# Experts gathered in pairs by 256-column products, and a down projection whose first unit waits for fewer hidden pairs

## What is computed

```python
def swiglu(h, w_in, w_out):
    g, u = jnp.split(jnp.einsum('bld,df->blf', h, w_in), 2, axis=-1)
    return jnp.einsum('blf,fd->bld', jax.nn.silu(g) * u, w_out)

def moe_swiglu(h, w_router, w_exp_in, w_exp_out):
    logits = jnp.einsum('bld,de->ble', h, w_router).astype(jnp.float32)
    top_v, top_i = lax.top_k(logits, TOP_K)
    gates = jax.nn.softmax(top_v, axis=-1)
    ...
    for e in range(N_EXPERTS):
        y = y + dense_gate[..., e:e + 1] * swiglu(h, w_exp_in[e], w_exp_out[e])
```

## Time and profile before

| What | us |
|---|---|
| median of 3 runs | 1950.88 (1950.7 to 1952.35) |
| the profiled execution: its own time | 1948.23 |
| its span, first to last instruction | 1946.5 |
| PE busy in the span | 1838.4 |
| DVE busy | 1338.6 |
| ACT busy | 1046.1 |

### The profile page before, as it was taken

The page is one execution under the profiler, slowest core; times in us unless marked ns, Lnnn a source line. Parts: engine busy times, 40 slices in busy tenths (PEclk is TensorE's granted clock), DMA queues, the critical chain, the costliest instruction groups (busy, mean ns, idle before and its releaser), DMA issues.

```text
span 1946.5 us, 25826 instructions
## 1 busy us (share of the span) xinstructions
PE 1838.4 (94%) x9949; PEld 1601.0 (82%) x9949; DVE 1338.6 (69%) x1160; ACT 1046.1 (54%) x924; POOL 85.1 (4%) x93
## 2 busy tenths in 40 slices
PE   6998988999889998987999999999999999999996
PEld 5997867999889988876888888888888888888885
DVE  3635554444355345536988889889888898888987
ACT  3443323333333442234677767776677767776775
POOL 2002120000000011211000000000000000000000
PEclk9998878999999978787999999999999999999998
DMA  7432134443462412135999999999999999999994
GB/s 241 140 123 55 35 95 132 146 147 115 120 190 87 152 41 54 45 103 201 338 364 326 355 340 344 367 331 353 364 330 353 328 354 368 327 351 334 353 357 146
DMA packets 267900, 452.62 MB, mean 233 GB/s; under 512 B 41258, under 2 KB 102946, under 8 KB 267832
## 3 DMA queue, kind: packets, MB, share of 16 engines
q1 hardware_dynamic: 266192, 448.83, 66.5%
q0 software_dynamic: 1376, 2.67, 0.7%
q10 hardware_dynamic: 264, 0.17, 0.1%
HBM read 440.66 MB, written 10.97 MB: 232 GB/s over the span
## 4 chain that ended last, share of the span: by engine, by line
PE 89%; DVE 7%; ACT 2%; issue 1%; DMA 1%; POOL 0%; SPq 0%; DVEq 0%; ACTq 0%
PE ps L1510 16%; PE ps L1511 16%; PE ps L2038 11%; PE ps L1505 8%; PE ps L1506 7%; PE ps L2053 5%; PE ps L1584 3%; PE ps L1969 3%; PE ps L1693 3%; PE ps L1678 2%; DVE cvt L1049 1%; PE ps L1984 1%; PE ps L2081 1%; DVE spL L944 1%; PE ps L1848 1%
## 5 line engine op out<-in xcount | busy, mean ns | idle before, releaser
L1401 DVE TENSOR_TENSOR spL<-ring,spH 128x2048 fp32r<-128x2048 f32 x339 | 771.5, 2292 | 113.0 <-ACT spH L873 112.9
L873 ACT ACTIVATE spH<-ring 128x2048 fp32r<-128x2048 f32 x339 | 648.6, 1916 | 124.9 <-PE ps L2053 64.8
L1510 PE MATMUL ps<-spH,XH 128*128 128x512 f32 x896 | 356.8, 398 | 1.5 <-DVE XL L1407 1.5
L1511 PE MATMUL ps<-spH,XL 128*128 128x512 f32 x896 | 352.0, 393 | 0.0
L944 DVE TENSOR_TENSOR spL<-ring,spH 128x2048 fp32r<-128x2048 f32 (+1 forms) x74 | 158.4, 2147 | 238.0 <-ACT spH L591 237.9
L1505 PE MATMUL ps<-hnH,spH 128*128 128x320 f32 x928 | 276.8, 313 | 13.7 <-DVE hnL L962 7.1
L1506 PE MATMUL ps<-hnL,spH 128*128 128x320 f32 x928 | 275.3, 311 | 0.0
L591 ACT ACTIVATE spH<-ring 128x2048 fp32r<-128x2048 f32 (+1 forms) x74 | 132.6, 1798 | 246.5 <-PE ps L1584 107.8
L2038 PE MATMUL ps<-spL,XH 128*128 128x512 f32 x896 | 241.8, 392 | 0.0
L1510 PEld LDWEIGHTS ps<-spH,XH 128*128 128x128 f32 x896 | 168.9, 188 | 37.8 <-issue 1.7
L2038 PEld LDWEIGHTS ps<-spL,XH 128*128 128x128 f32 x896 | 168.4, 188 | 36.8
(11 more groups left out here) (323 smaller groups left out, 2094.0 us busy)
## 6 DMA issues: line engine op xcount, KB each, us to landing
ring<-in_w_exp_in_dram SPq DMA_DIRECT2D x227, 1024.0 KB, 6.7
ring<-in_w_exp_out_dram SPq DMA_DIRECT2D x112, 1024.0 KB, 6.4
ring<-in_w_in_dram SPq DMA_DIRECT2D x28, 1024.0 KB, 5.7
ring<-in_w_ffn_in_dram SPq DMA_DIRECT2D x22, 1024.0 KB, 5.2
ring<-in_w_ffn_out_dram SPq DMA_DIRECT2D x16, 704.0 KB, 4.4
ring<-in_w_out_dram SPq DMA_DIRECT2D x8, 1024.0 KB, 5.0
out_dram<-ring SPq DMA_DIRECT2D x32, 256.0 KB, 2.6
ring<-in_state_hgrn_dram SPq DMA_DIRECT2D x16, 256.0 KB, 3.7
```

The lines of the kernel that those rows point to most:

```text
L873: A(esplit(j)[0], src, ACT.Copy).then_inc(S("hi_done"), 1)
L1401: V.tensor_tensor(lo, eslot(j)[0], hi.bitcast(F32), ALU.subtract).then_inc(S("split_done"), 1)
L1510: mm(out, x[0], w, start=start, stop=False)
L1511: return mm(out, x[1], w, start=False, stop=False)
```

## The change

Two experts are now gathered at once. `sel` has 256 columns, 128 for each expert of the pair, and `gather` has 40 products of 256 columns for two experts. Their output fills four banks instead of two, taken in the order 2, 3, 0, 1. The banks 0 and 1 still hold the last up chunk of the pair's second expert at that time, so that PE waits between the second and the third quarter for the multiplication of that chunk (`late`). ACT and DVE evacuate four quarters of 128 x 512 for a pair, as many as before for two experts. The loop's body is now a pair of experts (84 units), run four times; the gather stands in its second half alone, and `one_hot` makes six matrices instead of three, once for a pair.

In layer 0's down projection block m_ now adds up in bank (m_ + 4) mod 8. The first unit waits for ten pairs of hidden rows, the second for all eleven.

The core of the diff:

```diff
-        sel = put("sel", [P, 3, P], F32R)
+        sel = put("sel", [P, 3, 2 * P], F32R)
...
-        rank = put("rank", [P, NE + 1, 3])
+        rank = put("rank", [P, NE + 2, 3])
...
-        XH = put("XH", [P, KT, P], F32R, offset=base + 4 * KT * TOK)
-        XL = put("XL", [P, KT, P], F32R, offset=base + 8 * KT * TOK)
+        XH = put("XH", [P, KT, 2 * P], F32R, offset=base + 4 * KT * TOK)
+        XL = put("XL", [P, KT, 2 * P], F32R, offset=base + 8 * KT * TOK)
...
             def gathered(it):
 
-                for q in range(2):
-                    act.wait_ge(S("gath_mm"), it * 2 + (q + 1))
-                    A(XH[:, 4 * q:4 * q + 4],
-                      ps[:, 2 + q, :].rearrange("p (k n) -> p k n", k=4), ACT.Copy).then_inc(S("X_done"), 1)
-
-            def expert_act(it):
+                for q in range(4):
...
+                    expert_hi(it, j + AHEAD)
+                    if j == EU + UP_LAST[-1]:
                         gathered(it + 1)
...
-            with act.Fori(0, NE) as e:
-                expert_act(e)
+            with act.Fori(0, NE // 2) as e:
+                pair_act(e)
...
-                        V.tensor_tensor(xT[:, m], xT[:, m], ps[:, m, 0:TOK], ALU.add).then_inc(S("down_evac"), 1)
+                        V.tensor_tensor(xT[:, m], xT[:, m], ps[:, (m + 4) % 8, 0:TOK], ALU.add).then_inc(S("down_evac"), 1)
...
-                for t in range(3):
-                    i = V.tensor_scalar(sel[:, t], tabv("iota"), ranks[:, t:t + 1], None, ALU.is_equal)
+                for x in range(2):
+                    for t in range(3):
+                        i = V.tensor_scalar(sel[:, t, x * P:(x + 1) * P], tabv("iota"), ranks[:, x, t:t + 1], None,
+                                            ALU.is_equal)
                 i.then_inc(S("sel_done"), 1)
 
-            one_hot(rank[:, 0])
+            one_hot(rank)
...
             def gathered_lo(it):
...
-                for q in range(2):
-                    dve.wait_ge(S("X_done"), it * 2 + (q + 1))
-                    V.tensor_tensor(XL[:, 4 * q:4 * q + 4], ps[:, 2 + q, :].rearrange("p (k n) -> p k n", k=4),
-                                    XH[:, 4 * q:4 * q + 4].bitcast(F32), ALU.subtract).then_inc(S("XL_done"), 1)
-
-            def scatter_add(it, b, bank, added):
+                for q in range(4):
+                    dve.wait_ge(S("X_done"), it * 4 + (q + 1))
+                    V.tensor_tensor(XL[:, 2 * q:2 * q + 2], ps[:, (q + 2) % 4, :].rearrange("p (k n) -> p k n", k=2),
+                                    XH[:, 2 * q:2 * q + 2].bitcast(F32), ALU.subtract).then_inc(S("XL_done"), 1)
...
 
-                        V.tensor_copy(rk[:, 0], rank[:, bass.ds(nxt, 1), :].rearrange("p e t -> p (e t)")
-                                      ).then_inc(S("rk_done"), 1)
-                        dve.wait_ge(S("rk_done"), it * 2 + 2)
-                        one_hot(rk[:, 0])
+                        if x == 1:
+                            V.tensor_copy(rk[:, 0:2], rank[:, bass.ds(nxt, 2), :]).then_inc(S("rk_done"), 1)
+                            dve.wait_ge(S("rk_done"), it * 3 + 3)
+                            one_hot(rk)
...
-                    pe.wait_ge(S("hfL_done"), 11)
                     for m_ in range(8):
+                        bank = (m_ + 4) % 8
                         for half in range(2):
                             u = PLAN["down", 0] + 2 * m_ + half
+                            if m_ == 0:
+
+                                pe.wait_ge(S("hfL_done"), 10 if half == 0 else 11)
                             pe.wait_ge(S("hi_done"), u + 1)
                             wH, wL = unit(u, 11)
...
-                                high(ps[:, m_, 0:TOK], wH[:, k], (hfH[:, kk], hfL[:, kk]), start=kk == 0)
+                                high(ps[:, bank, 0:TOK], wH[:, k], (hfH[:, kk], hfL[:, kk]), start=kk == 0)
...
-            def gather(it):
+            def gather(it, late=None):
 
                 pe.wait_ge(S("sel_done"), it + 1)
-                for q in range(2):
-                    for k in range(4):
-                        kk = 4 * q + k
-                        out, d = ps[:, 2 + q, k * P:(k + 1) * P], slice(kk * P, (kk + 1) * P)
+                for q in range(4):
+                    if q == 2 and late:
+                        pe.wait_ge(late[0], late[1])
+                    for k in range(2):
+                        kk = 2 * q + k
+                        out, d = ps[:, (q + 2) % 4, k * 2 * P:(k + 1) * 2 * P], slice(kk * P, (kk + 1) * P)
                         for t in range(2):
                             mm(out, hkH[:, t, d], sel[:, t], start=t == 0, stop=False)
                             mm(out, hkL[:, t, d], sel[:, t], start=False, stop=False)
...
+            def pair_pe(it):
+
+                pe.wait_ge(S("XL_done"), it * 4 + 4)
+                for x, (j, (kind, c, i)) in itertools.product(range(2), enumerate(EXPERT_UNITS)):
+                    u, xs = x * EU + j, slice(x * P, (x + 1) * P)
+                    pe.wait_ge(S("hi_done"), it * PAIR + (U0 + u + 1))
+                    wH, wL = [x.rearrange("p (k n) -> p k n", k=4 if kind == "up" else 2) for x in esplit(u)]
...
+                    if u == EU + UP_LAST[-1]:
+
+                        pe.wait_ge(S("eh_done"), it * (2 * EC) + 2 * EC)
+                        gather(it + 1, (S("eh_done"), it * (2 * EC) + (2 * EC + 1)))
...
-            with pe.Fori(0, NE) as e:
-                expert_pe(e)
+            with pe.Fori(0, NE // 2) as e:
+                pair_pe(e)
```

More of the change, by code:

```diff
@@ L11 @@
+import itertools
 from contextlib import ExitStack
@@ L138 @@
 assert EU % AHEAD == 0 and EU % ERING == 0
+PAIR = 2 * EU
 UP_LAST = [EXPERT_UNITS.index(("up", c, 3)) for c in range(EC)]
@@ L918, in _ @@
                 with act.Fori(1, rounds) as r:
-                    with act.Fori(0, NE) as e:
-                        expert_act(act.snap(r * NE + e))
+                    with act.Fori(0, NE // 2) as e:
+                        pair_act(act.snap(r * (NE // 2) + e))
             tables(LN_EXP)
@@ L1412, in scatter_add @@
+            def scatter_add(it, x, b, bank, added):
                 t, q = divmod(b, 2)
                 n = TILES[t][1]
-                dve.wait_ge(S("scat_mm"), it * 6 + (b + 1))
+                dve.wait_ge(S("scat_mm"), it * 12 + (6 * x + b + 1))
                 V.scalar_tensor_tensor(out=ht[0:n, t, 512 * q:512 * q + 512], in0=ps[0:n, bank, :],
-                                       scalar=rk[0:n, 1, t:t + 1], in1=ht[0:n, t, 512 * q:512 * q + 512],
+                                       scalar=rk[0:n, 2, t:t + 1], in1=ht[0:n, t, 512 * q:512 * q + 512],
@@ L1417, in scatter_add, with pair_dve @@
                                        op0=ALU.mult, op1=ALU.add).then_inc(added, 1)
-            def expert_dve(e, it):
-                nxt = dve.snap(e + 1)
-                for p in range(EU):
+            def pair_dve(e, it):
+                nxt = dve.snap(e * 2 + 2)
+                for x, p in itertools.product(range(2), range(EU)):
+                    j = x * EU + p
                     if p == SELT_AT + 1:
-                        dve.wait_ge(S("selT_tr"), it + 1)
+                        dve.wait_ge(S("selT_tr"), it * 2 + (x + 1))
@@ L1465, in _ @@
             dve.wait_ge(S("yL_done"), 2)
-            with dve.Fori(0, NE) as e:
-                expert_dve(e, e)
+            with dve.Fori(0, NE // 2) as e:
+                pair_dve(e, e)
             rounds = dve.value_load(rndi[0:1, 0:1], min_val=1, max_val=MAXR)
@@ L1472, in _ @@
                     dve.drain()
-                    with dve.Fori(0, NE) as e:
-                        expert_dve(e, dve.snap(r * NE + e))
-            last = dve.snap(rounds * NE)
-            dve.wait_ge(S("rk_done"), last * 2 + 1)
+                    with dve.Fori(0, NE // 2) as e:
+                        pair_dve(e, dve.snap(r * (NE // 2) + e))
+            last = dve.snap(rounds * (NE // 2))
+            dve.wait_ge(S("rk_done"), last * 3 + 1)
             def finish(t):
@@ L1485, in _ @@
             for b in range(6):
-                scatter_add(last, b, 2 + b, S("moe_sum"))
+                scatter_add(last, 0, b, 2 + b, S("moe_sum"))
                 if b == 4:
@@ L1983, in _ @@
                                 kk = 11 * half + k
-                                m = mm(ps[:, m_, 0:TOK], wL[:, k], hfH[:, kk], start=False, stop=kk == 21)
+                                m = mm(ps[:, bank, 0:TOK], wL[:, k], hfH[:, kk], start=False, stop=kk == 21)
                             m.then_inc(S("used"), 1)
@@ L2090, in _ @@
                 with pe.Fori(1, rounds) as r:
-                    with pe.Fori(0, NE) as e:
-                        expert_pe(pe.snap(r * NE + e))
-            done = pe.snap(rounds * NE)
-            pe.wait_ge(S("yL_done"), done * 2 + 2)
+                    with pe.Fori(0, NE // 2) as e:
+                        pair_pe(pe.snap(r * (NE // 2) + e))
```

(2 more changed lines are left out.)

87 lines of the change are left out of this document (41 added, 46 removed).

## The result

| | before | after |
|---|---|---|
| median of the runs, us | 1950.79 (1947.58 to 1952.35, 4 runs) | 1930.66 (1928.28 to 1932.04, 4 runs) |
| profiled execution: span | 1946.5 | 1928.6 |
| profiled execution: its own time | 1948.23 | 1930.34 |

The ratio after to before is 0.991, with a 95% interval of 0.9889 to 0.9931. The forecast was 1930.4. The total agrees to 0.3 us; its parts do not, and most of what follows is about that.

A forecast was written before the change was run, and what follows sets the result against it. PE was taken as the bound, 89% of the 1946.5 us span; -16.2 + 0.4 + 1.7 - 6.4 = -20.5 us took 1948.23 to 1927.7, and 2.65 for the median gave 1930.4. Range: 1926 to 1938.

The forecast's parts named there:

- The price of 256 columns: In the gather, one product of 256 columns takes 0.119 us, between 0.110 and 0.147.
- Regular gathers: Inside the loop, four gathers of 4.76 us replace eight of 4.41 us on PE: -16.2 us.
- the wait in mid-gather: PE waits before a gather's third quarter for DVE's last chunk multiplication: 0.1 us for each of four, +0.4 us.
- ACT and DVE at the pair's end: 0: Four quarters instead of two come at once to ACT and DVE after a gather; idle time covers them: 0 us.
- The way into the loop: Ahead of the first expert product, DVE's extra one-hot matrices and `XL` quarters make PE start later: +1.7 us.
- Layer 0's down projection: -6.4: Between layer 0's up and down units, PE starts the first down unit without the 5.53 us pause: -6.4 us.
- The loop's code no longer stays where it is fetched from: Rival: the doubled body isn't held, so three jumps back wait for code, 7.2 us (shows as 2 to 9); chance 0.15.
- DMA becomes the bound: Rival: in the loop, 345 GB/s is the transfer ceiling, so the gathers give nothing: 1946.2 us; chance 0.07.
- A dear product: Rival: a 256-column gather product costs 0.25 us at full clock, making the kernel slower: +10.0 us, 1960.9; chance 0.04.
- only one part works: Rival: the layer-0 wait returns as another at the second down unit: -14.1 us, 1936.8; chance 0.06.

The follow-up runs named there:

- written-out kernel: The changed kernel with its four pairs written out on PE, ACT and DVE, with no jump back: 1924.51 us, ratio 0.9853.
- runs 1 and 2: 1: kernel before with layer 0's down projection changed alone, 1942.18 us; 2: changed kernel with that projection as before, 1938.57 us.
- runs 3 to 5: 3: kernel before, two experts per loop body, 1953.4 us; 4: changed kernel, four pairs written out, 1924.51 us; 5: kernel before, eight experts written out, 1949.54 us.

## Why the prediction was right in the total and wrong in one part

The total was right by luck: one term of 5.3 us was put at nothing, and other differences filled the place.

**The price of 256 columns** was right: 0.119 taken, 0.12 measured, the floor of 0.110 as read.

**Regular gathers and the wait in mid-gather** were right once the jumps are gone: -16.2 + 0.4 = -15.8 forecast, -15.4 measured in the written-out kernel. The wait costs 0.09 against 0.1.

**ACT and DVE at the pair's end: 0.** Right. Without the jumps PE is busy for the whole 250.30 us of a pair, which a late `XL` would not allow.

**The way into the loop** was right in size (+1.5 against +1.7) and in place. The first gather took 6.8 us, less than the 9.5 allowed, as the clock rose in the middle of it. That gained nothing, since DVE was the late one. What the prediction did not count is the clock behind it: the longer stop brought half clock back from 901.6 to 905.0. Against the kernel before this lost nothing, as there the first expert ran at half clock too, from 909.07 to 912.1.

**Layer 0's down projection: -6.4.** Right, to a tenth, also alone (5.86 us instead of 12.22).

**The rival that fired.** "The loop's code no longer stays where it is fetched from" had a chance of 0.15, at 2 to 9 us; it came, at 5.3. The step that failed is the argument against it: "It is 3.4 us ahead, which hides 2.4. The same holds for DVE and ACT, which have idle time there." The lead was right: 3.38 us at the first jump here (1150.0 to 1153.38). The price was wrong. 2.40 is what DVE stood still behind the loop, and it was taken for PE's. PE has a jump of its own behind the loop, in the same trace of the kernel before:

```profile
L2089 PEldq COMPARE_BRANCH  x1: 3692/3692/3692, 1925.2 to 1925.2; - x1
```

That is 3.69 us, more than the lead. In the changed kernel the three jumps back took 3.56 to 4.15 us, and 3.3 to 4.3 over all 18 jumps of the six kernels in which PE's body wasn't held (3.7 at the median). The full weights' queue isn't what makes them long: at 1925.2 no weights were being moved, and the jumps behind the loop took 3.4 to 3.7 us in all thirteen kernels. "The same holds for DVE" failed too. In the changed kernel DVE reaches its branch 2.2 us before its last split ends, but its sequencer goes on only 5.0 us after the branch, and DVE stands still three times:

```profile
DVE spL L1406 <- issue: 8.7, 3, 3.0
```

For ACT it held: ACT has no stop there.

The rule of the Trainium skill ("Runtime: NRT & Kernel Launch", Instruction fetch mechanics) had said this of PE: room for 2048 instructions, and a taken branch out of what is held waits for a fetch. The trace agrees: 1174 products and loads were held and 2268 were not, and q8's packets carry 0.46 MB in 28, 16 KB each, the block that the Trainium skill names. The room that the Trainium skill gives the other engines is 512 instructions. A pair has 283 recorded instructions on DVE, and the trace says that they are not held; ACT has 267 and goes on without a stop. The profile doesn't list all waiting instructions, so the count itself stays open.

**DMA becomes the bound** did not happen: the written-out kernel moved 353 GB/s over a pair with PE always busy. **A dear product** and **only one part works** are ruled out by the price and by runs 1 and 2.

**Why the total still fitted.** By its own stages the change gave 15.0 us where 20.5 were forecast. The profiled execution was 17.9 shorter, with 4.2 from the untouched stretch ahead of the selection and 1.2 lost before. The medians differ by 20.1; the interval of their ratio, 0.9889 to 0.9931, means 13.5 to 21.7 us and holds 15.0. The total alone would have hidden the jump; only the stage table and runs 3 to 5 show it.

What stays open: why a jump costs 1.4 us in one kernel and 3.5 in another, and what limits DVE's body. A body that holds a pair's gather but only one expert's units was not tried.

## What to carry to other kernels

Merging two passes of a loop to save work in each also doubles the code; compare the body with the largest that the trace shows running without instruction packets, on every engine, and not on the busiest alone. If it grows past that, write it out: here code that streams without a jump cost nothing (ratio 1.0001), and jumps back to a body that isn't held cost 1.5 to 2.5 us each, as the mean of a kernel's three (single ones 1.4 to 3.5). Where several engines must restart together, don't add their delays: removing one engine's alone gave 1.0 or 0.1 us, both 5.3.

## What the runs showed of the hardware that I had not expected

- A branch back cost PE's sequencer 0.2 us with a held body and 3.3 to 4.3 us with one that is not, of which its lead hid most: 1.8 to 2.5 us of kernel time were left a jump.
- DVE loses its pair's code too, at 144 busy instructions a pair, when PE's body is the one that looks long (1136 products). ACT, with 121, shows no stop.
- The first gather with 256 columns rose to full clock on its way (6.8 to 7.2 us), while the 128-column one stayed at half clock for all its 8.35 us. Behind it the clock fell to half again in the five kernels in which the first expert product came 3.9 to 4.4 us after the gather's last one had started, and not in the two where it came after 1.7 and 1.8 us; that alone was worth 1.7 us.
- Work that no edit touched took 321.8 to 326.7 us in twelve executions and 311.7 in the thirteenth: a stretch can differ by as much as the change itself brings.
